# Expert outputs scattered to their tokens' rows, and a new order of loads in the bridge and the join

## The reference

```python
x = x + g1x * mixer_output(...)                   # bridge: output projection, residual
h = modulate(rmsnorm(x, norm2_g), sh2x, sc2x)     # bridge: rows of h2, router
# router: best of 4 groups, best 2 of its 8 experts, weights from two softmaxes
order = jnp.argsort(expert_ids)                   # 2048 assignments, sorted by expert
buf = zeros(...).at[dest].set(tok[token_of])      # padded to blocks of 128 rows
yb = lax.map(expert_block, ...)                   # silu(x @ gate) * (x @ up) @ down
y = yb[dest] * weights
x = x + g2x * segment_sum(y, token_of)            # join
```

## Time and profile before

| | |
|---|---|
| median of 3 runs | 4262.29 us (4260.09 to 4262.51) |
| the profiled execution | 4256.27 us, span 4254.6 us |
| PE busy | 3777.7 us (89%) |
| DVE busy | 2248.2 us (53%) |
| ACT busy | 1514.1 us (36%) |
| POOL busy | 1122.4 us (26%) |
| DMA moved | 639.31 MB, mean 150 GB/s |

### The profile page before, as it was taken

One profiled execution on the slowest core, in us unless ns is written; L12 is line 12 of the kernel. 1 busy time (PEld: TensorE's weight loads), 2 busy tenths in 40 slices (PEclk: granted clock), 3 DMA queues, 4 the chain that ended last, 5 costly groups with the idle time before them and its releaser, 6 DMA issues. The chain is left out here.

```text
span 4254.6 us, 44454 instructions
## 1 busy us (share of the span) xinstructions
PE 3777.7 (89%) x16978; PEld 2979.4 (70%) x16978; DVE 2248.2 (53%) x2583; ACT 1514.1 (36%) x1912; POOL 1122.4 (26%) x597
## 2 busy tenths in 40 slices
PE   4899988486899999669988699999879899999998
PEld 1788877455777787556666467777667688888886
DVE  6468547736788888665534222222236453353345
ACT  3321211334677777424120322222232332332233
POOL 2221220125111111222320212222034344444443
PEclk8899997697999999769987899999989999999999
DMA  4411124635899999823410211111044333333323
GB/s 150 121 44 69 68 92 131 225 138 200 337 400 400 401 402 400 327 83 117 149 70 25 107 43 67 67 68 53 33 178 144 134 94 95 99 94 95 98 85 109
DMA packets 161971, 639.31 MB, mean 150 GB/s; under 512 B 20824, under 2 KB 44216, under 8 KB 145680
## 3 DMA queue, kind: packets, MB, share of 16 engines
q1 hardware_dynamic: 133920, 554.29, 36.2%
q10 hardware_dynamic: 18096, 52.96, 3.2%
q0 software_dynamic: 9792, 29.81, 1.9%
HBM read 533.37 MB, written 103.63 MB: 150 GB/s over the span
## 5 line engine op out<-in xcount | busy, mean ns | idle before, releaser
L3402 POOL TENSOR_TENSOR t_wl<-t_raw,t_wh 128x1024 fp32r<-128x1024 f32 (+1 forms) x176 | 397.4, 2261 | 543.7 <-ACT t_wh L3454 543.5
L99 PE MATMUL m_b<-b_high,m_high 128*128 128x512 f32 x960 | 414.5, 432 | 28.3 <-ACT m_ob L2350 19.1
L100 PE MATMUL m_b<-b_rest,m_high 128*128 128x512 f32 x960 | 393.4, 410 | 0.0
L101 PE MATMUL m_b<-b_high,m_low 128*128 128x512 f32 x960 | 384.7, 401 | 0.0
L2321 POOL TENSOR_TENSOR m_high<-m_raw,m_one 128x1024 fp32r<-128x1024 f32 x60 | 117.6, 1960 | 915.0 <-PE m_b L101 860.5
L99 PE MATMUL t_b<-b_high,t_wh 128*128 128x512 f32 x768 | 303.1, 395 | 18.2 <-POOL t_wl L3402 18.0
L100 PE MATMUL t_b<-b_rest,t_wh 128*128 128x512 f32 x768 | 300.8, 392 | 0.0
L101 PE MATMUL t_b<-b_high,t_wl 128*128 128x512 f32 x768 | 300.6, 391 | 0.0
L3454 ACT ACTIVATE t_wh<-t_raw 128x1024 fp32r<-128x1024 f32 (+1 forms) x176 | 175.6, 999 | 339.8 <-PE t_b L101 287.0
L99 PE MATMUL zs_z<-zs_hs,zs_high 128*128 128x512 f32 (+1 forms) x632 | 239.8, 379 | 28.0 <-POOL zs_hs L277 28.0
L99 PEld LDWEIGHTS m_b<-b_high,m_high 128*128 128x128 f32 x960 | 187.5, 195 | 90.6 <-ACT m_ob L2350 19.6
(11 more groups left out here) (650 smaller groups left out, 8910.9 us busy)
## 6 DMA issues: line engine op xcount, KB each, us to landing
moe_raw<-in_expert_w SPq DMA_DIRECT2D x79, 2048.0 KB
ex_raw<-in_expert_w SPq DMA_DIRECT2D x39, 2048.0 KB
t_raw<-in_w_ff SPq DMA_DIRECT2D x128, 512.0 KB, 3.4
m_raw<-in_w_ug SPq DMA_DIRECT2D x60, 512.0 KB, 4.5
yrows<-ex_y ACTq DMA_DIRECT2D x38, 512.0 KB
zs_raw<-in_ada_w SPq DMA_DIRECT2D x32, 512.0 KB
gates<-m_ob SPq DMA_DIRECT2D x32, 512.0 KB, 2.9
me_g<-gates SPq DMA_DIRECT2D x32, 512.0 KB, 3.8
```

Source lines behind the costliest of these rows:

```text
L99: nc.tensor.matmul(out, w[0], x[0], start=first, stop=False)
L100: nc.tensor.matmul(out, w[0], x[1], start=False, stop=False)
L101: return nc.tensor.matmul(out, w[1], x[0], start=False, stop=last)
L3402: self.nc.gpsimd.tensor_tensor(self.wl[u % self.NW][:, 0:m], self.raw[u % 2][:, 0:m], self.wh[u % self.NW][:, 0:m].bitcast(F32), ALU.subtr ...
```

## The change

1. `yrows` now has a row for each token and each of its two experts (2 * 1024 rows, plus 256 for padding). `slots` has rows of 8 integers: column 0 the token to gather, columns 1 to 7 the row of `yrows` to write. The fill of `yrows` is dropped; `slots` is filled with token 0 and a padding row.
2. In the expert loop the store of ScalarE is dropped. GpSimd loads the same 128 rows of `slots` once more (`into`), waits for the copy of the block's result and scatters it.
3. The join's rows are plain loads by SP; the first product of `mix` is done by ScalarE (`weigh`).
4. Bridge: SP issues residuals ahead of weights, weights one unit nearer, expert weights at the end; rows 6 and 7 are transposed ahead of the count.

```diff
@@ -993,11 +993,10 @@
...
                     if n == 2:
-                        sp.wait_ge(C["blanked"], 1)
-                        sp.dma_start(R["yrows"][NE * SLOT:NBLK * SLOT, :].rearrange("(p b) (x n) -> p (b x) n", p=P, n=P),
-                                     blank[:].unsqueeze(1).broadcast_to([P, KD * (NBLK - NE), P])).then_inc(C["cleared"], 16)
-                        sp.dma_start(R["slots"].rearrange("(p b c) n -> p b (c n)", p=P, b=10),
-                                     blank[:, 0:80].bitcast(I32).unsqueeze(1).broadcast_to([P, 10, 80])).then_inc(C["cleared"], 16)
+                        sp.wait_ge(C["blanked"], 2)
+                        for x in range(2):
+                            sp.dma_start(R["slots"].rearrange("(c x p) n -> x p c n", p=P, x=2)[x],
+                                         pads[:, x, :].unsqueeze(1).broadcast_to([P, (NBLK + 2) // 2, 8])).then_inc(C["cleared"], 16)
                     if n == Z_MV:
@@ -1011,7 +1010,9 @@
...
             def _(pool):
-                nc.gpsimd.memset(blank[:], 0.0).then_inc(C["blanked"], 1)
+                nc.gpsimd.iota(pads[:], pattern=[[P, 2], [0, 8]], base=2 * SEQ, channel_multiplier=1).then_inc(C["blanked"], 1)
+                pool.wait_ge(C["blanked"], 1)
+                nc.gpsimd.memset(pads[:, :, 0:1], 0).then_inc(C["blanked"], 1)
                 Z.fill(pool)
@@ -1229,22 +1230,19 @@
...
         gates(1)
-        weight(4)
         for u in range(self.NU):
...
                 outs(7)
-            if u + 5 < self.NU:
-                weight(u + 5)
             if u >= 2 and u + 1 < self.NU:
                 residual(u + 1)
-            if u == 7:
-                sp.wait_ge(self.left, NCX)
-                for j in range(2):
-                    sp.dma_start(self.raw[j][:], A["expert_w"][j]).then_inc(self.raw_in[j], 16)
+            if u + 4 < self.NU:
+                weight(u + 4)
             if u >= 12:
                 rows(u - 12)
+            if u >= 14:
+                sp.dma_start(self.raw[u - 14][:], A["expert_w"][u - 14]).then_inc(self.raw_in[u - 14], 16)
         for ch in range(4, NCX):
@@ -1270,7 +1268,9 @@
...
 
-        G.iota(self.tok[:], pattern=[[P, NCX], [0, 16]], base=0, channel_multiplier=1).then_inc(self.noted, 1)
+        G.iota(self.tok[:], pattern=[[P, NCX], [SEQ, 2], [0, 8]], base=0, channel_multiplier=1).then_inc(self.noted, 1)
+        pool.wait_ge(self.noted, 1)
+        G.iota(self.tok[:, :, :, 0:1], pattern=[[P, NCX], [0, 2], [0, 1]], base=0, channel_multiplier=1).then_inc(self.noted, 1)
         G.iota(self.sloti[:], pattern=[[1, P]], base=1, channel_multiplier=0).then_inc(self.noted, 1)
@@ -1410,10 +1410,10 @@
...
         rows(5)
+        rows(6)
+        rows(7)
         count()
-        rows(6)
         listing(0)
-        rows(7)
         listing(1)
@@ -1880,8 +1881,9 @@
...
                         nc.gpsimd.indirect_dma_start(out=R["slots"], out_offset=bass.IndirectOffsetOnAxis(ap=C["dest"][:, c, k:k + 1], axis=0),
-                                                     in_=B.tok[:, c, :], in_offset=None).then_inc(scattered, 16)
+                                                     in_=B.tok[:, c, k, :], in_offset=None).then_inc(scattered, 16)
                 pool.wait_ge(scattered, 16 * 2 * NCX)
+                nc.gpsimd.tensor_tensor(pace[:], C["ones"][:, 0:1], C["ones"][:, 0:1], ALU.add).then_inc(paced, 1)
                 nc.gpsimd.tensor_tensor(carry[:], C["ones"][:, 0:1], C["ones"][:, 0:1], ALU.add).then_inc(carried, 1)
@@ -1890,6 +1892,14 @@
...
                         gather(b + 2, j)
+                        pool.wait_ge(stored[j], i * 16)
+                        pool.dma_start(into[j][:], R["slots"][bass.ds(b * SLOT, SLOT), :]).then_inc(into_in, 16)
+                        pool.wait_ge(into_in, b * 16 + 16)
+                        pool.wait_ge(taken, b + 1)
+                        pool.wait_ge(paced, b + 1)
+                        nc.gpsimd.tensor_tensor(pace[:], C["ones"][:, 0:1], C["ones"][:, 0:1], ALU.add).then_inc(paced, 1)
+                        nc.gpsimd.indirect_dma_start(out=R["yrows"], out_offset=bass.IndirectOffsetOnAxis(ap=into[j][:, 1:2], axis=0),
+                                                     in_=y[j][:], in_offset=None).then_inc(stored[j], 16)
                 for j in range(2):
@@ -1967,7 +1977,6 @@
...
                         high(u, m % 3, m // 3, x_)
-                act.wait_ge(C["cleared"], 32)
                 n = count(act)
@@ -1989,8 +1998,6 @@
...
                         high("o", 0, b + 2, 1)
-                        act.wait_ge(taken, b + 1)
-                        act.dma_start(R["yrows"][bass.ds(b * SLOT, SLOT), :], y[j][:]).then_inc(stored[j], 16)
                 for j in range(2):
@@ -2102,19 +2109,35 @@
...
         self.got, self.x_in = s.sems("j_got", self.NR), s.sems("j_x_in", 2)
-        (self.g_in, self.own, self.mixed, self.turned, self.added, self.squared, self.summed, self.meant, self.rooted, self.inverted, self.spread, self.scaled,
+        (self.g_in, self.own, self.weighed, self.mixed, self.turned, self.added, self.squared, self.summed, self.meant, self.rooted, self.inverted, self.spread, self.scaled,
          self.h_high, self.ended, self.stored) = (s.sem("j_" + n) for n in (
-             "g_in", "own", "mixed", "turned", "added", "squared", "summed", "meant", "rooted", "inverted", "spread", "scaled", "h_high", "ended", "stored"))
+             "g_in", "own", "weighed", "mixed", "turned", "added", "squared", "summed", "meant", "rooted", "inverted", "spread", "scaled", "h_high", "ended", "stored"))
         self.h_low = s.sems("j_h_low", 2)
 
-    def load(self, sp):
-        for c in range(2):
-            cut = slice(c * BANK, (c + 1) * BANK)
-            sp.dma_start(self.x[:, :, cut], self.R["x1"].rearrange("k p t -> p k t")[:, :, cut]).then_inc(self.x_in[c], 16)
-            if c == 0:
-                sp.dma_start(self.gf[:], self.A["final_g"]).then_inc(self.g_in, 16)
-                for n, g in enumerate(("g_mix", "g_mlp", "g_ple", "g_final")):
-                    sp.dma_start(self.gains[:, n, :], self.A[g]).then_inc(self.g_in, 16)
+    def load(self, sp, between):
+        def rows(t):
+            if t >= self.NR:
+                sp.wait_ge(self.mixed, t - self.NR + 1)
+            for k in range(2):
+                sp.dma_start(self.r[t % self.NR][k][:], self.R["yrows"][k * SEQ + t * P:k * SEQ + (t + 1) * P, :]).then_inc(self.got[t % self.NR], 16)
+
+        def residual(c):
+            sp.dma_start(self.x[:, :, self.cut(c)], self.R["x1"].rearrange("k p t -> p k t")[:, :, self.cut(c)]).then_inc(self.x_in[c], 16)
+
+        rows(0)
+        residual(0)
+        rows(1)
+        rows(2)
+        sp.dma_start(self.gf[:], self.A["final_g"]).then_inc(self.g_in, 16)
+        for n, g in enumerate(("g_mix", "g_mlp", "g_ple", "g_final")):
+            sp.dma_start(self.gains[:, n, :], self.A[g]).then_inc(self.g_in, 16)
+        rows(3)
+        rows(4)
+        residual(1)
+        rows(5)
+        between()
+        rows(6)
+        rows(7)
 
@@ -2125,13 +2148,6 @@
...
 
-    def gather(self, pool, t):
-        if t >= self.NR:
-            pool.wait_ge(self.mixed, t - self.NR + 1)
-        for k in range(2):
-            self.nc.gpsimd.indirect_dma_start(out=self.r[t % self.NR][k][:], out_offset=None, in_=self.R["yrows"],
-                                              in_offset=bass.IndirectOffsetOnAxis(ap=self.dest[:, t, k:k + 1], axis=0)).then_inc(self.got[t % self.NR], 16)
-
     def cut(self, c):
@@ -2140,11 +2156,8 @@
...
     def gpsimd(self, pool, halve):
-        for t in range(NCX):
-            self.gather(pool, t)
-            if t == self.NR - 1:
-                halve(0)
-                halve(1)
+        halve(0)
+        halve(1)
         for k in range(KD):
@@ -2157,12 +2170,9 @@
...
         def mix(t):
-            r0, r1 = self.r[t % self.NR]
             dve.wait_ge(self.got[t % self.NR], 32 * (t // self.NR + 1))
-            if t >= 2:
-                dve.wait_ge(self.turned, t - 1)
-            st.then(V.tensor_scalar(self.y[t % 2][:], r0[:], self.wt[:, t, 0:1], None, ALU.mult))
-            V.scalar_tensor_tensor(self.y[t % 2][:], r1[:], self.wt[:, t, 1:2], self.y[t % 2][:], ALU.mult, ALU.add).then_inc(self.mixed, 1)
+            dve.wait_ge(self.weighed, t + 1)
+            V.scalar_tensor_tensor(self.y[t % 2][:], self.r[t % self.NR][1][:], self.wt[:, t, 1:2], self.y[t % 2][:], ALU.mult, ALU.add).then_inc(self.mixed, 1)
 
@@ -2220,6 +2230,12 @@
...
 
+        def weigh(t):
+            act.wait_ge(self.got[t % self.NR], 32 * (t // self.NR + 1))
+            if t >= 2:
+                act.wait_ge(self.turned, t - 1)
+            S.activation(self.y[t % 2][:], self.r[t % self.NR][0][:], ACT.Identity, bias=0.0, scale=self.wt[:, t, 0:1]).then_inc(self.weighed, 1)
+
         def square(t):
@@ -2234,9 +2250,14 @@
...
 
-        for t in range(5):
+        for t in range(3):
+            weigh(t)
```

(14 more changed lines are left out.)

21 lines of the change are left out of this document (11 added, 10 removed).

## The result

The changed kernel took 4322.0 us in the median of five runs (4298.46 to 4324.65), the kernel before 4262.29: a ratio of 1.0129, 95% interval 1.0099 to 1.0159. The change makes it slower by 1.3%. The profiled execution of the changed kernel took 4298.46 us with a span of 4296.8; its other four took 4319 to 4325, and no trace shows these. Stage by stage, the two profiled executions (spans 4254.6 and 4296.8) differ as follows. The marks are the first and last rows of a few tiles; for each stretch the forecast's term stands beside it.

The account below looks back on a forecast made before the run. Bounds: TensorE and DMA engines both full in the expert loop, a ring of waits in the bridge, TensorE in the join. Terms 0 - 17 + 59 + 1 - 10 = +33 on 4262.3 gave 4295 us, range 4236 to 4350.

Parts of the forecast that it names:

- likeliest case: Whole kernel: 19.3 to 21.2 us a block in the expert loop, 4270 to 4340 us in all, chance 0.52.
- Clearing, 0: Start of kernel: dropped yrows fill, slots fill in 32-byte pieces and two more iotas cost 0, bound -2 to +5.
- Bridge, -17: Attention output and router: residual loads no longer queue behind blocked SP, TensorE sets the pace; -17.2 us, bounds -8 to -22.
- Expert loop, +59: Expert loop: 21.6 us chain from block end to gathered rows makes 20.0 us a block, not 18.36; bounds 0 to +163.
- the first rival: Expert loop: GpSimd's slack and landings shortened by DMA holes hide everything; cost 0 to 18 gives 4236 to 4254, chance 0.25.
- the second: Expert loop: GpSimd's own ring rules, each small load paying for 128 rows ahead of it; 4340 to 4425 us, chance 0.15.
- The third rival: Expert loop: gaps lower TensorE's granted clock; at 0.9, 21.0 us a block and 4331 us, inside the forecast's range.
- A loop cost of 0.72 us a block: Expert loop: where the hidden-loop side decides, 26 us in all, with the two landings summing to less than 17.1 us.
- a ring of 22.9 us: Expert loop: GpSimd's own ring if each small load takes 9.6 us behind 128 rows, the upper bound of +163 us.
- End of the loop, +1: After the last block: a scatter lands 4.3 us or more after its issue, costing +1 us.
- Join, -10: Join: plain loads and ScalarE's first product save 10 us, between 0 (rows 5 to 7 late behind SP's waits) and -13.
- the carrying over of the profiled difference to the median: Whole kernel: profiled execution 4256.3 us, median 4262.3; a difference was assumed to carry over as it is.

Follow-up runs that it names:

- run 11: run 10 with the join's gains loaded ahead of its first rows and slots filled by 512 pieces of 416 bytes instead of 6400 of 32: 4236.2 us.
- run 9: The changed kernel measured a second time without an edit: 4305.1 us.
- run 10: run 5 with the load of the destinations for block b + 1 also issued before GpSimd waits for the copy of block b: 4236.9 us.
- runs 8 and 4: Changed kernel, scatter replaced by a plain store to two fixed places, sum over experts left out: 4293.0 us on GpSimd's queue, 4307.9 us on ScalarE's.
- run 3: Changed kernel with GpSimd's second slots load per block dropped, the destinations copied from the tile the same block's gather had used: 4314.6 us.
- run 5: Changed kernel with the gather for block b + 3 and the slot load for b + 4 issued before GpSimd waits for the copy of b: 4250.5 us.
- run 6: run 5 with the join's five small gain loads issued ahead of its first rows: 4250.2 us.
- runs 2 and 5: First: changed kernel with the slot load for block b + 3 ahead of the wait for the copy of b, 4261.7 us. Second: see run 5.

## Why the prediction was right, and where not

The forecast was 4295 us, range 4236 to 4350, slower with a chance of 0.67. The measured median is 4322.0, inside the range and inside the likeliest case's own 4270 to 4340. Median against median the change cost 59.7 us, not 33; profile against profile, where the terms can be checked one by one, 42.2.

**Clearing, 0.** Right that the fill costs nothing that can be seen: SP's rows of 475 us stand 1.2 us sooner than before. The 2.2 us that the first sum came later arise behind it, and their cause is open (run 11).

**Bridge, -17.** Right in mechanism and size: -16.8 from first to last sum, and -17.3 when done alone. The row stores behind the expert weights gave nothing back; the stretch behind the last sum became shorter by 1.8 (1.0 alone).

**Expert loop, +59.** Right in mechanism: end of block, copy, tiny add, scatter, slot load, gather, rows. From the changed kernel's rows the chain is 1.3 to the copy's end, 1.69 to the scatter, 1.0 for its issue, 7.97, 1.23 and 8.69, together 21.9, where the forecast had 21.6; (21.9 + 18.36) / 2 = 20.1 us, measured 20.32 on average. That the sum came so close is luck in part, for three of its terms were off and cancelled. The gather was taken at 10.6 and took 8.7 (9.7 in run 9), while the DMA engines had holes, as the first rival had said. Copy to scatter was taken at 0.45 and took 1.69, as the load of the destinations was late in 23 blocks, as the second had said. The add and gap between slot load and gather were taken at 0.35, the shortest seen, and took 1.23; the last section shows what lengthens this add. The slot load, 7.9 from a single pair of rows, was 7.97 on average (6.67 in run 9), but with a spread from 5 to 12 that one pair can't show. In all the pitch rose by 1.9 us over 34 blocks, and the loop's first four blocks together took 1.6 us less, where the forecast had 1.64 over 36.

**What the rivals were worth.** That the loop hides the work is refuted for this order of GpSimd (TensorE waits 54.0 us) and true for another (run 10). The Trainium skill, DMA: Bandwidth & Descriptors, section Issuing engines are not separate DMA queues, holds in this sense: the transfer is no dearer for being started by GpSimd (a plain store with GpSimd's order kept took 4293.0 us in all from GpSimd's queue and 4307.9 from ScalarE's, runs 8 and 4). What cost nearly all of those 63 us was that GpSimd waits in order, and that a load needed by TensorE stood behind the wait. GpSimd's own ring was not the bound in the changed kernel (run 3), but it was the next one (run 5). The third rival was real, but small. The clock was granted at 0.98 from 1080 to 1740 us, not at its 0.9, and at 0.93 in the two worst of the loop's 50-us stretches. TensorE was busy for 606.01 us with 32.5 blocks there, 18.66 a block, against 18.32 before (658.48 for 35.9). Only one block of TensorE lies in the ring of two, so half of those 0.3 us reach the pitch: (21.9 + 18.7) / 2 = 20.3, as measured. That makes some 6 of the 63 us, an estimate. The forecast's sum had no term for it.

Two prices of the rivals don't follow from their own terms. A loop cost of 0.72 us a block needs the two landings to sum to 16.7 us, not 17.1 (2 * 19.08 - 18.36 - 3.1). And a ring of 22.9 us gives 4262 + 163 - 26 = 4399, not 4425, which leaves out the 26 us of gains. Neither moves the forecast or its range.

**End of the loop, +1.** +1.9: a scatter must land before the join begins.

**Join, -10.** -8.3. Right that the gains hold the beginning (VectorE's first instruction stands 16.7 us after the start, 17.8 before). The rows of chunk 1, which come at 13.0 and hold it next (run 6), weren't in the forecast. Too hopeful for the second half: ScalarE's products waited 4.0 and 5.2 us for rows behind SP's waits, the bound that the forecast had named.

**Size.** The step that was mis-sized is the carrying over of the profiled difference to the median: the changed loop has no fixed pitch, and four of the kernel's first five executions took 21 to 26 us longer than the profiled one. Why those four were longer is open (run 9). The changed kernel spreads over 26 and 24 us in its two measurements, the kernel before over 16 and 17 in the same two. A median cost of +44.7 (run 9) and +59.7 was measured for one and the same change.

## What to carry to other kernels

A transfer that moves to another engine takes its wait with it: list what is queued behind that wait, and put every load that the bound engine needs ahead of it, by a block if the buffers allow. A small load behind scattered or gathered rows took 5 to 17 us here while its engine did nothing, so the order of four transfers decided 68 to 85 us (4305 or 4322 to 4237) with nearly the same bytes. When such a chain is cut, look for the next one: the first two cuts (runs 2 and 5) each uncovered a transfer that had been hidden by the one before, and only after the third (run 10) did TensorE wait for nothing.
